# Hybrid layer with mixture-of-experts lookup: a second half of one token block leaves the dense up products, and 120 of 128 up tiles run early

## The chip, the cores and the metric

The kernel runs on one core of one Trainium2 chip. The metric is the device time of one execution in microseconds (us), median of several.

## The reference

One layer on 512 tokens of width 1024 in float32. A mixer (sliding-window attention, gated delta rule) and its output projection come first and are not touched here. Then comes the expert lookup, `peer`:

```python
q = (xt @ w_q).reshape(T, PEER_HEADS, 2, PEER_HALF)
s = jnp.einsum('thpc,hpnc->thpn', q, sub_keys)
s_top, i_top = lax.top_k(s, PEER_TOPK)
cand_s = s_top[:, :, 0, :, None] + s_top[:, :, 1, None, :]      # 16 x 16 sums
cand_i = i_top[:, :, 0, :, None] * N_KEYS + i_top[:, :, 1, None, :]
best_s, pos = lax.top_k(cand_s, PEER_TOPK)
idx, gate = take(cand_i, pos), softmax(best_s)
act = gelu(einsum('tkd,td->tk', u_tab[idx], x))
out = einsum('tk,tkd->td', act * gate, v_tab[idx])
```

Each token picks 8 x 16 = 128 of 16384 experts (128 x 128 pairs of keys i, j). Each expert is a row u and a row v of 1024 numbers.

## The kernel before, in words

The 512 tokens are four blocks of 128. Block 0 takes the way of single rows: for each of its 128 picks a gather brings [128 tokens, u and v] (1 MB, `Gathered.fetch`, line 1804), VectorE makes the dot with the token (`dot`, 1811) and, with gelu and gate, adds the scaled v row (`add`, 1828). Dots and adds are steps that `pair_steps` deals out, by a list of rates, to the batches of the routing stage and to the tiles of the last stage.

Blocks 1 to 3 take the dense way: all 128 x 128 experts' dots, with a gate of zero where an expert isn't picked. An **up tile** is the product of 128 u rows (one key j, all i) with the tokens; each operand is split in a high and a low part, so it is 8 x 3 matmuls. ScalarE makes the high part of u (`split_u`), GpSimd or VectorE the low part by subtraction (`u_low`, 2008), TensorE multiplies by the token columns (2097, 2098, then 2102 once the low part is there). A **down tile** is the product of gated activations with 128 v rows, 18 matmuls of 512 columns (2426 to 2428) over 384 tokens.

For half of block 1 (its first 64 tokens, NS = 64) the up dots don't come from the dense way but from gathered u rows (class `UpRows`): the 64 tokens' 128 picks are folded into 64 gathers of [128, 1024] (512 KB, 1878) and 64 VectorE dots (1885). The folding needs the second half of the indices and gates moved between partitions by two transfers (1868, 1869) and the tokens' rows repeated by a matmul (2125). Their activations times gates go in as the values of the gate matrix. So up tiles have 320 columns (TU = 384 - 64).

The work is three stages. The **routing stage** (about 408 to 905 us) runs the first FIRST = 27 up tiles (DRAM gets their gelus, 160 KB each) while VectorE selects the picks of blocks 1 and 2 (`Selection.part`, 13 parts a block; the order of blocks is 1, 2, 3, 0). Then 48 batches of 8 tokens build the gate matrix: VectorE writes two one-hots (2238), ScalarE scales one (2177), TensorE multiplies them (2119), ScalarE evicts and every second batch SP stores 1 MB. Between the two halves of a batch run more up tiles, `ups_in[n]`; in a batch VectorE also does a part of a selection (`beside`), the dots on gathered rows (DOTS = 2 a batch from batch 0), and from batch LATE = 32 steps of block 0. GpSimd goes in program order through `pool_low` (the subtractions) and the gathers; a gather into one of four row places waits until the dot that used the place is done. EARLY = 104 up tiles are made in this stage.

The **last stage** first runs its 24 up tiles beside down tiles (two tiles behind, a loop of three bodies of 8), then 104 down tiles alone, with gelus loaded back (L2370), v tiles in four places (2352) and gate tiles of 768 KB. Steps of block 0 run at 3.1 and then 1.5 a tile. At the end h is added and stored; h itself is loaded again in one transfer of 2 MB. SP issues all these loads in one order, each after the wait for its place.

The lines that set the order of a batch on TensorE and on GpSimd:

```python
for n in range(NB_):
    for i in range(BT // 4):
        for t in ups_of[n][i:i + 1]:
            up(t)
        gate_products(n, i)
```
```python
for n in range(LATE):
    for k in range(fetched, min(NS, fetched + (DOTS if n else 2 * DOTS))):
        up_rows.fetch(pool, k)
        fetched += 1
    for t in ups_of[n]:
        pool_low(t)
```

Of the kernel before, what the change touches and what calls it, by code (L numbers as in the profile page):

```python
# [51 lines left out]
EARLY = 104  # L52
NU = 4
TD = T - P
NS = 64
NR = P // NS
# [1242 lines left out]
class Selection:  # L1299
# [4 lines left out]
    def __init__(self, nc, sem, own, mem, scores, sgate, sidx):  # L1304
# [17 lines left out]
        self.idxf = part_of("top_index_f", [P, 2, PH, TOPK])  # L1322
# [9 lines left out]
        self.zsum = part_of("rt_z", [P, PH])  # L1332
        self.row0_made = part_of("row_starts", [P, TOPK])
        self.rowd = part_of("row_lengths", [P, TOPK])
        self.moved = part_of("shared_index_moved", [P, P], U32)
# [6 lines left out]
    def place_constants(self, dve, bank):  # L1342

        link = self.link(dve)
        self.iota, self.row0 = bank[:, 0:NK], bank[:, NK:NK + TOPK]
        self.step = bank[:, 256:512].rearrange("p (q h a) -> p q h a", q=2, h=PH)
        link(self.nc.vector.tensor_copy(self.iota, self.iota_made[:]))
        link(self.nc.vector.tensor_copy(self.row0, self.row0_made[:]))
# [7 lines left out]
    def second(self, r, w):  # L1356
        return self.top[:, 1, :, 0:w].unsqueeze(2).broadcast_to([P, PH, r, w])
# [7 lines left out]
    def constants(self, pool):  # L1365
# [14 lines left out]
    def part(self, dve, b, part):  # L1380
# [27 lines left out]
        elif part == 5:  # L1408
            off = 0
# [14 lines left out]
        elif part == 6:  # L1424
# [5 lines left out]
            link(nc.vector.tensor_copy(self.zsum[:].unsqueeze(2), self.best[:, :, 0:1]))  # L1430
            nc.vector.tensor_tensor(self.best[:], self.best[:], self.bc(self.zsum[:].unsqueeze(2), TOPK),
                                    ALU.subtract).then_inc(self.subbed, 1)
        elif part == 7:

            nc.vector.tensor_copy(self.posf[:], self.pos[:])
            link(nc.vector.tensor_copy(self.idxf[:], self.idx[:]))
            nc.vector.tensor_copy(self.step[:, :, :, 0:1], self.idxf[:, :, :, 0:1])
            link(nc.vector.tensor_tensor(self.step[:, :, :, 1:], self.idxf[:, :, :, 1:], self.idxf[:, :, :, :TOPK - 1],
# [5 lines left out]
            link(nc.vector.tensor_tensor(self.wide[:], self.flat(self.posf).unsqueeze(2).broadcast_to([P, HA, TOPK]),  # L1444
                                         self.row0.unsqueeze(1).broadcast_to([P, HA, TOPK]), ALU.is_ge))
        elif part in (8, 11):
            for h in range(PH):
                v = self.wide[:, h * TOPK:(h + 1) * TOPK, :]
                t = nc.vector.tensor_tensor(v, v, self.step[:, 0 if part == 8 else 1, h].unsqueeze(1)
                                            .broadcast_to([P, TOPK, TOPK]), ALU.mult)  # L1450
            link(t)
        elif part == 9:

            link(nc.vector.tensor_reduce(self.packed[:], self.wide[:], AX, ALU.add))
            link(nc.vector.tensor_copy(self.words[:], self.packed[:]))
            nc.vector.tensor_scalar(self.words2[:], self.words[:], 63, None, ALU.bitwise_and)
            link(nc.vector.tensor_scalar(self.words[:], self.words[:], 6, None, ALU.logical_shift_right))
            nc.vector.tensor_copy(self.small[:, 0, :], self.words[:])
            link(nc.vector.tensor_copy(self.column[:], self.words2[:]))
# [1198 lines left out]
```

## Time and profile before

| | |
|---|---|
| median of 3 runs | 1532.24 us (1531.07 to 1534.07) |
| the profiled execution | 1532.0 us, its span 1530.3 us |
| TensorE busy | 1451.6 us, 95% of the span |
| VectorE busy | 1275.8 us, 83% |
| ScalarE busy | 829.3 us, 54% |
| GpSimd busy | 504.4 us, 33% |
| DMA | 420.49 MB, mean 275 GB/s over the span |
| granted TensorE clock | 0.985 of full in the mean |

PE is TensorE, PEld its weight loads, DVE VectorE, ACT ScalarE, POOL GpSimd, SP the queue that issues most transfers. Busy times of PE count overlapping matmuls once. The DMA share is the time that packets took on the core's 16 DMA engines; it goes a little over 1 when packets of two queues overlap on an engine.

### The profile page before, as it was taken

The numbers are of one execution on the slowest core, as the hardware profiler recorded it, in microseconds if no ns is written. First come the engines' busy times: TensorE is split into PE (matmuls) and PEld (weight loads), VectorE is DVE, ScalarE is ACT, GpSimd is POOL, SyncE is SP. The second block draws the span as 40 slices with busy tenths as digits, with TensorE's granted clock in tenths as the row PEclk, the third lists the DMA queues.
The fourth block names the chain that finished last, engine by engine and source line by source line (L and its number), as shares of the span: only waits on it lengthen the run. The fifth ranks groups of instructions, "written<-read, shape, count | busy, mean of one in ns | idle before, by whom it ended". The sixth has DMA issues, their size and how long they took to land.

```text
span 1530.3 us, 25321 instructions
## 1 busy us (share of the span) xinstructions
PE 1451.6 (95%) x9438; PEld 1311.3 (86%) x9438; DVE 1275.8 (83%) x2444; ACT 829.3 (54%) x1571; POOL 504.4 (33%) x425
## 2 busy tenths in 40 slices
PE   7999699999999999999998989999989999999999
PEld 6898578779999999998998979999868888888887
DVE  4538778675799899999868949999979999998996
ACT  4453454133244667777767754444546565655653
POOL 4111620010177867776731103222212222221210
PEclk9999999999999999999999999999999999999999
DMA  5230001321266898999999999999999999999993
GB/s 185 93 98 1 8 30 61 135 97 70 75 192 231 283 321 301 346 340 311 334 353 386 384 350 352 380 380 324 386 408 410 410 409 411 409 411 409 410 390 105
DMA packets 168440, 420.49 MB, mean 275 GB/s; under 512 B 12897, under 2 KB 100097, under 8 KB 151681
## 3 DMA queue, kind: packets, MB, share of 16 engines
q1 hardware_dynamic: 125632, 234.06, 42.3%
q0 software_dynamic: 27712, 167.82, 28.3%
q10 hardware_dynamic: 14976, 17.05, 3.1%
q8 instruction: 73, 1.20, 0.3%
q14 instruction: 47, 0.38, 0.1%
HBM read 372.44 MB, written 46.40 MB: 274 GB/s over the span
## 4 chain that ended last, share of the span: by engine, by line
PE 47%; DVE 15%; DMA 6%; POOL 2%; issue 1%; ACT 1%; SPq 0%; ACTq 0%; DVEq 0%; POOLq 0%
PE bank L2426 7%; PE bank L2428 7%; PE bank L2427 7%; PE banks L2426 3%; PE banks L2428 3%; PE banks L2427 3%; PE bank L2102 3%; PE bank L2097 3%; PE bank L2098 3%; DVE pair_rows L1885 2%; DMA u_raw<-in_peer_u 2%; DVE onehot_i L2238 2%; DVE onehot_j L2238 2%; PE bank L2414 2%; PE bank L2415 2%; PE bank L2416 2%
## 5 line engine op out<-in xcount | busy, mean ns | idle before, releaser
L2097 PE MATMUL bank<-x_hi,u_split 128*128 128x320 f32 x832 | 253.4, 316 | 1.6 <-ACT u_split L2157 1.6
L2098 PE MATMUL bank<-x_lo,u_split 128*128 128x320 f32 x832 | 246.8, 309 | 0.0
L1804 POOL DMA_INDIRECT scores<-in_peer_uv,pair_index x86 | 106.3, 1236 | 389.0 <-DVE pair_sum L1828 387.9
L2473 ACT ACTIVATE act_tile<-onehots 128x384 f32<-128x384 f32 x128 | 124.3, 971 | 82.1 <-DVE act_lo L2515 78.4
L2097 PEld LDWEIGHTS bank<-x_hi,u_split 128*128 128x128 f32 x832 | 157.9, 190 | 2.6 <-issue 2.6
L2098 PEld LDWEIGHTS bank<-x_lo,u_split 128*128 128x128 f32 x832 | 157.2, 189 | 0.0
L2102 PE MATMUL bank<-x_hi,u_split 128*128 128x320 f32 x832 | 142.1, 312 | 13.2 <-POOL u_split L2008 13.2
L2102 PEld LDWEIGHTS bank<-x_hi,u_split 128*128 128x128 f32 x832 | 128.1, 190 | 15.3 <-POOL u_split L2008 15.3
L2008 POOL TENSOR_TENSOR u_split<-u_raw,u_split 128x1024 fp32r<-128x1024 f32 x41 | 98.8, 2412 | 79.9 <-DVE u_split L2008 58.2
L2426 PE MATMUL bank<-v_hi,act_hi 128*128 128x512 f32 x304 | 119.5, 393 | 1.5 <-DVE v_lo L2502 1.4
L2428 PE MATMUL bank<-v_hi,act_lo 128*128 128x512 f32 x304 | 119.1, 392 | 0.0
L2427 PE MATMUL bank<-v_lo,act_hi 128*128 128x512 f32 x304 | 118.3, 389 | 0.0
L2119 PE MATMUL bank<-onehot_j,onehot_gated 128*128 128x128 f32 x768 | 100.7, 279 | 13.4 <-ACT onehot_gated L2177 11.8
L1828 DVE SCALAR_TENSOR_TENSOR pair_sum<-scores,pair_c,pair_sum 128x1024 f32<-128x1024 f32 x86 | 110.1, 1282 | 1.5
L2502 DVE TENSOR_TENSOR v_lo<-v_raw,v_hi 128x1024 fp32r<-128x1024 f32 x76 | 92.7, 1220 | 21.4 <-ACT v_hi L2457 21.4
L2119 PEld LDWEIGHTS bank<-onehot_j,onehot_gated 128*128 128x128 f32 x768 | 96.1, 195 | 15.3 <-issue 14.2
L1804 POOL DMA_INDIRECT pair_rows<-in_peer_uv,pair_index x42 | 55.4, 1318 | 158.6 <-DVE pair_sum L1828 157.9
L2008 POOL TENSOR_TENSOR u_split<-u_raw_more,u_split 128x1024 fp32r<-128x1024 f32 x41 | 98.8, 2414 | 25.2 <-ACT u_split L2157 24.9
L1811 DVE SCALAR_TENSOR_TENSOR scores<-scores,mix 128x1024 f32<-128x1024 f32 x86 | 104.7, 1217 | 1.1 <-DMA scores<-in_peer_uv,pair_index 1.1
L2177 ACT ACTIVATE onehot_gated<-onehot_i,rt_smallT 128x128 f32<-128x128 f32 x320 | 101.3, 391 | 1.7 <-DVE onehot_i L2238 1.3
L2157 ACT ACTIVATE u_split<-u_raw_more 128x1024 fp32r<-128x1024 f32 x52 | 55.0, 1058 | 74.0 <-PE bank L2102 41.8
L2457 ACT ACTIVATE v_hi<-v_raw 128x1024 fp32r<-128x1024 f32 x76 | 80.0, 1053 | 23.1 <-DMA v_raw<-in_peer_v 22.8
(433 smaller groups left out, 4055.7 us busy)
## 6 DMA issues: line engine op xcount, KB each, us to landing
v_raw<-in_peer_v SPq DMA_DIRECT2D x128, 512.0 KB, 10.8
u_raw<-in_peer_u SPq DMA_DIRECT2D x64, 512.0 KB, 7.1
u_raw_more<-in_peer_u SPq DMA_DIRECT2D x64, 512.0 KB, 7.1
gates<-gate_stage SPq DMA_DIRECT2D x24, 1024.0 KB, 7.4
onehots<-gates SPq DMA_DIRECT2D x32, 768.0 KB, 11.4
early_gelus<-early_gelu ACTq DMA_DIRECT2D x104, 160.0 KB, 5.4
gelu_tile<-early_gelus SPq DMA_DIRECT2D x104, 160.0 KB, 11.2
w_raw<-in_w_in SPq DMA_DIRECT2D x9, 1024.0 KB, 5.2
```

The lines of the kernel that those rows point to most:

```text
L1804: pool.indirect_dma_start(self.slot(k), None, self.table, bass.IndirectOffsetOnAxis(ap=self.sidx[:, k:k + 1], axis=0)).then_inc(self.lande ...
L1811: self.nc.vector.scalar_tensor_tensor(row, row, 1.0, self.xn0, ALU.mult, ALU.mult, accum_out=self.s[:, at:at + 1]).then_inc(self.dots, 1)
L1828: self.nc.vector.scalar_tensor_tensor(total, self.slot(k)[:, D:], self.c[:, at:at + 1], total, ALU.mult, ALU.add).then_inc(self.summed, 1)
L2008: return on.tensor_tensor(ul[:, n % 2, :], u_raw[n % NU], uh[:, n % 2, :].bitcast(F32), ALU.subtract)
L2097: nc.tensor.matmul(out, uh[:, q, w], m.xh[:, k, P + NS:], start=(k == 0), stop=False)
L2098: nc.tensor.matmul(out, uh[:, q, w], m.xl[:, k, P + NS:], start=False, stop=False)
L2102: t = nc.tensor.matmul(out, ul[:, q, w], m.xh[:, k, P + NS:], start=False, stop=(k == KD - 1))
L2119: t = nc.tensor.matmul(banks.bank(g)[:, q * NK:(q + 1) * NK], og[:, n % RING, 4 * i + q, :], oj[:, n % RING, 4 * i + q, :], start=True, st ...
L2426: nc.tensor.matmul(bank[:], ah[:, s, w], v_hi[:, c], start=first, stop=False)
L2427: nc.tensor.matmul(bank[:], ah[:, s, w], v_lo[:, c], start=False, stop=False)
L2428: t = nc.tensor.matmul(bank[:], al[:, s, w], v_hi[:, c], start=False, stop=last)
L2473: nc.scalar.activation(af[n % 2][:], gt[:, it % 2, :, jj], ACT.Copy).then_inc(gate_cols, 1)
```

## The change

All 128 tokens of block 1 now take their up dots from gathered rows (NS = 128), so up tiles have 256 columns. Every token has a partition of its own, so the moving transfers, the repeated rows and the folding are gone; 128 gathers and 128 dots are made, five a batch in batches 0 to 24, through eight row places instead of four. 120 up tiles are early; 26 come before batch 0, batches 0 to 24 have three or two (67 in all), later ones one, four come last. In the selection several operands (places, packed words, the second keys' sums, the maximum) move from SBUF to PSUM, eight multiplications become one, some copies go. Block 2's picks are turned before batch 0, all 16 batches of block 1 come at the end. The four first v tiles are loaded in batches 40, 42, 44 and 46 instead of together at 32, and h in four parts.

The last stage keeps eight up tiles and has 120 down tiles alone; the steps of block 0 run at 1.7 a tile there. By the rates, 15 adds and 21 gathers of block 0 are placed in the routing stage both before and now; in the last stage 35 adds fell on the 24 up tiles and 78 on the 104 others, now 10 and 103.

```diff
-EARLY = 104
+EARLY = 120
-NS = 64
-NR = P // NS
+NS = P
...
-    LAST = 5
+    LAST = 4
     LATE = 2 * NBT
-    ups_in = [1 if n >= LATE or n % 4 == 3 else 2 for n in range(NB_)]
+    DOTS_FIRST, DOTS = 4, 5
+    LAST_DOT = (NS - 1 - DOTS_FIRST) // DOTS
+    ups_in = [1 if n > LAST_DOT else 2 if n % 3 == 2 else 3 for n in range(NB_)]
+    def ups_at(n, i):
+        return ups_of[n][0:1] if i == 0 else ups_of[n][1:]
...
-        beside[i * 29 // len(left)] = what
+        beside[i if i < sel.PARTS else sel.PARTS + (i - sel.PARTS) * 16 // sel.PARTS] = what
-    turned_at = {2: 1, 3: ready_at[3] + 1}
-    DOTS_FIRST, DOTS = 4, 2
+    turned_at = {2: -1, 3: ready_at[3] + 1}
-    COEFS = LAST_DOT + 2
+    COEFS = LAST_DOT + 4
+    V_AT = [NB_ - 8, NB_ - 6, NB_ - 4, NB_ - 2]
...
-                fetched = len(up_rows.slots)
+                SLOTS = len(up_rows.slots)
+                fetched = SLOTS - 2
                 for t in range(1, FIRST):
                     pool_low(t)
                     if t == TURN_1 + 2:
-                        up_rows.move(pool, sel)
-                    if t == TURN_1 + 3:
-                        up_rows.wait_moved(pool)
+                        pool.wait_ge(up_rows.chosen, 1)
                         for k in range(fetched):
                             up_rows.fetch(pool, k)
                 for n in range(LATE):
-                    for k in range(fetched, min(NS, fetched + (DOTS if n else 2 * DOTS))):
-                        up_rows.fetch(pool, k)
-                        fetched += 1
-                    for t in ups_of[n]:
+                    for i, t in enumerate(ups_of[n]):
                         pool_low(t)
+                        if i == 0:
+                            if n == 0:
+                                pool.wait_ge(sel.pairs_ready, 2)
+                            for k in range(fetched, min(NS, DOTS_FIRST + DOTS * n + SLOTS)):
+                                up_rows.fetch(pool, k)
+                                fetched += 1
...
-        self.iota, self.row0 = bank[:, 0:NK], bank[:, NK:NK + TOPK]
+        self.iota, self.posf, self.zsum = bank[:, 0:NK], bank[:, NK:2 * NK], bank[:, NK:NK + PH]
         self.step = bank[:, 256:512].rearrange("p (q h a) -> p q h a", q=2, h=PH)
+        self.packed, self.seconds = bank[:, 256:384], self.step[:, 1]
+        self.words = self.packed.bitcast(U32)
...
-            for h in range(PH):
-                v = self.wide[:, h * TOPK:(h + 1) * TOPK, :]
-                t = nc.vector.tensor_tensor(v, v, self.step[:, 0 if part == 8 else 1, h].unsqueeze(1)
-                                            .broadcast_to([P, TOPK, TOPK]), ALU.mult)
-            link(t)
+            v = self.wide[:].rearrange("p (h a) k -> p h a k", h=PH)
+            link(nc.vector.tensor_tensor(v, v, self.step[:, 0 if part == 8 else 1].unsqueeze(2)
+                                         .broadcast_to([P, PH, TOPK, TOPK]), ALU.mult))
...
         up_slots = [more[:, i, half * D:(half + 1) * D] for i in range(2) for half in range(2)]
+        up_slots += [rows[:, b, half * D:(half + 1) * D] for b in (1, 2) for half in range(2)]
-        rates = [2.0] * (P // 8) + [1.0, 2.0] + [3.1] * (NK - EARLY - 2) + [1.5] * EARLY
+        rates = [2.0] * (P // 8) + [1.0, 2.0] + [3.1] * (NK - EARLY - 2) + [1.7] * EARLY
...
+    H_AT = [NMT + 12 + 20 * b for b in range(TB)]
-                    if n == NMT + 4:
+                    if n in H_AT:
+                        b = H_AT.index(n)
                         sp.wait_ge(up_done, NMT)
-                        sp.dma_start(h[:], h_dram).then_inc(h_in, 16)
+                        sp.dma_start(h[:, b, :], h_dram[:, b, :]).then_inc(h_in, 16)
```

On GpSimd, in the batches: before, two gathers stood in a row, then the subtractions of one or two tiles (u_split is the tile of high and low parts, pair_rows and scores hold the row places; "x4" is four instructions in a row):

```order
L2008 TENSOR_TENSOR u_split<-u_raw,u_split 128x1024 [waits early_u_hi]
L1878 DMA pair_rows<-in_peer_uv,up_index 128x1024 [waits up_dots] x2
L2008 TENSOR_TENSOR u_split<-u_raw_more,u_split 128x1024 [waits early_u_hi] x2
L1878 DMA pair_rows<-in_peer_uv,up_index 128x1024 [waits up_dots] x2
L2008 TENSOR_TENSOR u_split<-u_raw,u_split 128x1024 [waits early_u_hi] x2
```

Now, from the last subtractions of batch 0 to the gathers of batch 2:

```order
L1989 TENSOR_TENSOR u_split<-u_raw_more,u_split 128x1024 [waits early_u_hi]
L1989 TENSOR_TENSOR u_split<-u_raw,u_split 128x1024 [waits early_u_hi] x2
L1856 DMA scores<-in_peer_uv,up_index 128x1024 [waits up_dots] x4
L1856 DMA pair_rows<-in_peer_uv,up_index 128x1024 [waits up_dots]
L1989 TENSOR_TENSOR u_split<-u_raw_more,u_split 128x1024 [waits early_u_hi] x2
L1989 TENSOR_TENSOR u_split<-u_raw,u_split 128x1024 [waits early_u_hi]
L1856 DMA pair_rows<-in_peer_uv,up_index 128x1024 [waits up_dots] x3
L1856 DMA scores<-in_peer_uv,up_index 128x1024 [waits up_dots] x2
```

Five gathers now stand together after the first subtraction of a batch, and up to three subtractions lie between two such groups.

On VectorE, batch 1 before (the one-hots, a selection part, two dots):

```order
L2238 TENSOR_TENSOR onehot_i<-bank,rt_smallT 128x1024
L2238 TENSOR_TENSOR onehot_j<-bank,rt_smallT 128x1024
L1393 MAX_INDEX top_index<-top,scores 128x8 x8
L1395 MATCH_REPLACE scores<-top,scores 128x128 x8
L1885 SCALAR_TENSOR_TENSOR pair_rows,up_s<-pair_rows,banks 128x1024 [waits rows_landed2,dve_in_order]
L1885 SCALAR_TENSOR_TENSOR pair_rows,up_s<-pair_rows,banks 128x1024 [waits rows_landed3]
```

and batch 1 now:

```order
L2222 TENSOR_TENSOR onehot_i<-bank,rt_smallT 128x1024
L2222 TENSOR_TENSOR onehot_j<-bank,rt_smallT 128x1024
L1387 MAX_INDEX top_index<-top,scores 128x8 x8
L1389 MATCH_REPLACE scores<-top,scores 128x128 x8
L1863 SCALAR_TENSOR_TENSOR pair_rows,up_s<-pair_rows,banks 128x1024 [waits rows_landed1,dve_in_order]
L1863 SCALAR_TENSOR_TENSOR pair_rows,up_s<-pair_rows,banks 128x1024 [waits rows_landed2]
L1863 SCALAR_TENSOR_TENSOR pair_rows,up_s<-pair_rows,banks 128x1024 [waits rows_landed3]
L1863 SCALAR_TENSOR_TENSOR scores,up_s<-scores,banks 128x1024 [waits rows_landed4]
L1863 SCALAR_TENSOR_TENSOR scores,up_s<-scores,banks 128x1024 [waits rows_landed5]
```

The batch has the same one-hots and the same selection part, and five dots where it had two.

## Rows read from the trace of the kernel before

**Rows 1.** The page: busy time of each engine, share of the span, instructions.

```profile
PE 1451.6 (95%) x9438; PEld 1311.3 (86%) x9438; DVE 1275.8 (83%) x2444; ACT 829.3 (54%) x1571; POOL 504.4 (33%) x425
```

**Rows 2.** Windows by stage: length, busy times, PEclk, DMA share, GB/s.

```profile
408.00:515.00 107.00, 103.03 (x681) 101.07 (x680) 97.87 (x383) 49.93 (x74) 75.46 (x38) 0.98 0.67 220
515.00:784.00 269.00, 259.52 (x1863) 257.94 (x1863) 249.84 (x648) 194.45 (x440) 190.47 (x117) 0.99 0.94 322
784.00:905.00 121.00, 104.69 (x746) 102.32 (x745) 94.20 (x104) 80.52 (x200) 14.79 (x15) 0.97 1.03 383
905.00:1090.00 185.00, 182.51 (x1001) 163.93 (x1000) 167.64 (x226) 92.08 (x143) 52.39 (x36) 1.00 0.95 358
1090.00:1140.00 50.00, 44.48 (x186) 36.01 (x185) 41.49 (x62) 24.72 (x36) 9.96 (x8) 0.93 1.02 412
1140.00:1490.00 350.00, 350.00 (x1532) 287.37 (x1531) 329.88 (x483) 208.86 (x291) 77.78 (x64) 1.00 1.02 408
1490.00:1530.00 40.00, 37.08 (x163) 30.14 (x161) 27.91 (x39) 13.35 (x19) 0.00 (x0) 1.00 0.32 114
```

**Rows 3.** DMA issues from 1140 to 1490 us: KB each, median us to landing.

```profile
v_raw<-in_peer_v SPq DMA_DIRECT2D x86, 512.0 KB, 12.1
```

**Rows 4.** Timeline of PE, 320 columns: start us, us, the instruction.

```profile
601.11 0.31 PE L2098 MATMUL bank<-x_lo,u_split 128*128 128x320 f32 x1
...
603.17 0.31 PE L2098 MATMUL bank<-x_lo,u_split 128*128 128x320 f32 x1
```

**Rows 5.** Timeline of PE, query projection at 256 columns.

```profile
362.08 0.28 PE L1558 MATMUL banks<-x_lo,w_oq_h 128*128 128x256 f32 x1
...
364.48 0.28 PE L1557 MATMUL banks<-x_hi,w_oq_h 128*128 128x256 f32 x1
```

**Rows 6.** Timeline of PE, down products at 512 columns.

```profile
1203.78 0.39 PE L2426 MATMUL banks<-v_hi_late,act_hi 128*128 128x512 f32 x1
...
1205.84 0.40 PE L2426 MATMUL bank<-v_hi,act_hi 128*128 128x512 f32 x1
```

**Rows 7.** Gate products: line 2119 (first and last start), then timeline, batch 32.

```profile
L2119 PE MATMUL bank<-onehot_j,onehot_gated x768: 271/275/550, 515.1 to 883.1; 128*128 128x128 f32 x192
...
784.34 1.95 PE L2119 MATMUL bank<-onehot_j,onehot_gated 128*128 128x128 f32 x16
```

**Rows 8.** Timeline of DVE and POOL: a copy at two places.

```profile
421.19 0.21 DVE L1430 COPY rt_z<-best 128x8 f32<-128x8 f32 x1
...
564.96 4.70 POOL L2008 TENSOR_TENSOR u_split<-u_raw_more,u_split 128x1024 fp32r<-128x1024 f32 x2
...
568.27 1.41 DVE L1430 COPY rt_z<-best 128x8 f32<-128x8 f32 x1
```

**Rows 9.** Timeline of DVE inside a batch: a dot and two one-hots.

```profile
562.39 1.22 DVE L1885 SCALAR_TENSOR_TENSOR pair_rows<-pair_rows,banks 128x1024 f32<-128x1024 f32 x1
...
563.53 1.22 DVE L2238 TENSOR_TENSOR onehot_i<-bank,rt_smallT 128x1024 f32<-128x1024 f32 x1
...
564.66 1.21 DVE L2238 TENSOR_TENSOR onehot_j<-bank,rt_smallT 128x1024 f32<-128x1024 f32 x1
```

**Rows 10.** Timeline of POOL: two gathers between u_low subtractions.

```profile
593.16 2.42 POOL L2008 TENSOR_TENSOR u_split<-u_raw,u_split 128x1024 fp32r<-128x1024 f32 x1 [0.30 <-ACT u_split L2157]
595.74 0.95 POOL L1878 DMA_INDIRECT pair_rows<-in_peer_uv,up_index  x1 [0.15 <-issue]
596.99 0.94 POOL L1878 DMA_INDIRECT pair_rows<-in_peer_uv,up_index  x1 [0.30 <-issue]
597.94 2.42 POOL L2008 TENSOR_TENSOR u_split<-u_raw,u_split 128x1024 fp32r<-128x1024 f32 x1
```

**Rows 11.** Windows of 10 us, same columns as rows 2.

```profile
590.00:600.00 10.00, 10.00 (x74) 10.00 (x73) 9.96 (x10) 7.99 (x19) 9.21 (x6) 1.00 1.01 372
1110.00:1120.00 10.00, 10.00 (x45) 8.19 (x45) 9.51 (x15) 4.97 (x7) 1.91 (x2) 1.00 1.02 421
```

More of the change, by code:

```diff
@@ L1408, in part @@
         elif part == 5:
+            link(nc.vector.tensor_copy(self.seconds, self.top[:, 1]))
             off = 0
@@ L1841, with __init__ @@
 class UpRows:
-    def __init__(self, nc, sem, slots, landed, xs, table, take):
+    def __init__(self, nc, sem, slots, landed, xs, table, strips):
         self.nc, self.slots, self.xs, self.table = nc, slots, xs, table
         self.landed = landed
-        self.chosen, self.moved, self.dots, self.gelus, self.coefs = (sem(n) for n in (
-            "up_chosen", "up_moved", "up_dots", "up_gelus", "up_coefs"))
-        self.idx, self.gate = take("up_index", [P, NS], U32), take("up_gate", [P, NS])
-        self.s, self.c = take("up_s", [P, NS]), take("up_c", [P, NR, NS])
+        self.chosen, self.dots, self.gelus, self.coefs = (sem(n) for n in (
+            "up_chosen", "up_dots", "up_gelus", "up_coefs"))
+        self.idx, self.gate = strips[0], strips[1]
+        self.s, self.c = strips[2], strips[3]
     def choose(self, dve, sel):
@@ L1981, in routing @@
             banks.add(("small", 1), "dve")
+    banks.add(("small", 2), "dve")
     for n, (b, k) in enumerate(BATCHES):
         for i in range(BT // 4):
-            for t in ups_of[n][i:i + 1]:
+            for t in ups_at(n, i):
                 banks.add(("up", t), "act")
@@ L2000, in routing @@
         smallT = sb("rt_smallT", [P, 2, 3, P])
-        ownT = sb("rt_ownT", [P, 3, NS])
+        ownT = [m.mem.over(f"own{i}", [P, NS], "x_hi", F32, 4 * T * i) for i in range(3)]
         small = sel.small
@@ L2434, in body @@
                         up(it, jj)
-                        if jj >= LAG or not isinstance(it, int):
-                            down(it * BODY + jj - LAG, jj - LAG + BODY, first=isinstance(it, int) and jj == LAG)
+                        if jj >= LAG:
+                            down(jj - LAG, jj - LAG, first=jj == LAG)
                 body(0)
-                with pe.Fori(1, NM) as it:
-                    body(it)
                 for n in range(NMT - LAG, NK):
@@ L2618, in hybrid_layer @@
         m.xs = two
-        up_rows = UpRows(nc, sem, up_slots, pairs_of_0.landed[:4], two[:].rearrange("p h d -> p (h d)"),
+        up_rows = UpRows(nc, sem, up_slots, pairs_of_0.landed + [sem(f"up_landed{i}") for i in range(2)], two[:].rearrange("p h d -> p (h d)"),
                          a["peer_uv"].rearrange("e (two d) -> (e two) d", two=2),
-                         lambda name, shape, dt=F32: mem.take(name, shape, dt))
+                         [mem.over(name, [P, NS], "x_hi", dt, 4 * T * (3 + i))[:] for i, (name, dt) in enumerate(
+                             [("up_index", U32), ("up_gate", F32), ("up_s", F32), ("up_c", F32)])])
         m.v_raw = [mem.over(f"v_raw{i}", [P, D], "selection", F32, 4 * D * i)[:] for i in range(3)]
```

120 lines of the change are left out of this document (48 added, 72 removed).

## The prediction, made before the changed kernel ran

> **What bounds the kernel now.** I read the page first. TensorE is busy 95% of the span and VectorE 83% [rows 1], so the question is which stage has room for work moved between engines. The windows by stage answer it [rows 2]. From 408 to 515 us (early up tiles and two selections) VectorE is busy 97.9 of 107 us and the DMA queues are at 0.67. From 515 to 784 us (batches 0 to 31) TensorE is busy 259.5 of 269 and DMA at 0.94. From 784 to 905 us DMA is at 1.03 and TensorE drops to 104.7 of 121: this stretch waits for loads. From 905 to 1090 us (24 up tiles beside down products) TensorE is nearly full. From 1140 to 1490 us (down products alone) TensorE is busy all 350 us, **and** DMA is at 1.02 with 408 GB/s. So the last stage has two bounds at once. Its v loads take 12.1 us in the middle from issue to landing [rows 3], with four places and a tile time near 4.1 us. A queue with room would not hold them so long.
>
> The start-to-start times of matmuls give TensorE's prices, since a row's own duration overlaps its neighbour. At 320 columns 14 matmuls take 603.17 - 601.11 = 2.06 us, 0.147 each [rows 4]; at 256 columns, in the query projection, 20 take 364.48 - 362.08 = 2.40 us, 0.120 each [rows 5]; at 512 columns nine take 2.06 us, 0.229 each [rows 6]. The first gate products of batch 0 start at 515.1 us and those of batch 32 at 784.3 [rows 7], 269.2 us or 8.4 a batch.
>
> **The change, part by part.**
>
> *Narrower up tiles.* 24 matmuls a tile: 24 x 0.147 = 3.52 us before, 24 x 0.120 = 2.88 after. For 128 tiles that takes 82 us off TensorE. It is worth time only where TensorE is what ends last.
>
> *The start.* TensorE now has 26 tiles ahead of batch 0 instead of 27, 26 x 2.88 = 75 us from about 411, plus some 5 us of waiting while GpSimd issues six gathers in a row (6 x 1.25 us, below), plus the first tile of batch 0: its first gate products could start at 494. VectorE must have finished block 2's selection by then. It ended at 515 with 9 us of idling in the window [rows 2], and now waits less, since six rows are fetched ahead. The copy of eight elements that takes 0.21 us alone took 1.41 us later, beside two GpSimd subtractions [rows 8]; the new PSUM operands take several such operations out of each selection, and the eight small multiplications become one. I put 12 us on both selections together, so about 494 as well. Taken: 495, a gain of **20** (between 10, if none of the long operations gets shorter, and 25).
>
> *Batches 0 to 24.* Here lies the price. The 64 further rows add 64 gathers of 512 KB (33.6 MB) and 64 VectorE dots. All 124 dots after the first four now come five to a batch, with 67 up tiles in 25 batches (2.68 each). Per batch:
> TensorE: 2.68 x 2.88 + 1.8 (16 gate-product records, [rows 7]) = 9.5 us.
> VectorE: two one-hots of 1.13 us, five dots of 1.14 [rows 9], and one part of a selection. Before, 32 batches held 249.8 us of VectorE work; less 64 one-hots (72.6) and 60 dots (68.4) that leaves 108.8 for 26 parts, 4.2 each with the long operations in it; I take 3.4. Sum 11.4, falling to about 10.8 from batch 13.
> GpSimd: u_low 2.41 us a tile, gathers 1.25 us from start to start and 0.95 for the last [rows 10]. With three tiles 3 x 2.41 + 0.15 + 4 x 1.25 + 0.95 = 13.3, with two 10.9; 17 and 8 batches give 12.5 in the mean, without one wait.
> DMA: 2.68 u loads (1.405 MB), five gathers (2.621), half a gate store (0.524), 2.68 gelu stores of 128 KB (0.351): 4.90 MB. At 372 GB/s, which ten saturated us of the same kind of traffic moved at a share of 1.01 [rows 11], it is 13.2 us; at the 421 GB/s of the best window shown, 11.6; at 322/0.94 = 343 GB/s, what rows 2 give per full share in batches 0 to 31, 14.3.
> So three resources lie between 11.4 and 13.2, and TensorE is no longer one of them. I take **13.0** a batch (ends: 12.5 from GpSimd, 14.3 from DMA): 325 us.
>
> *Batches 25 to 31* have one tile and no dot: 5.3 us each, as the one-tile batches after 784 had (3.52 + 1.78) before loads stopped them; 37 us. Batch 32 then starts at 495 + 325 + 37 = 857, against 784: **+73**, the 20 us of the start taken off.
>
> *Batches 32 to 47 and the last tiles.* DMA-bound [rows 2] and with almost the same bytes: 16 pair steps a side as before, one tile fewer at the end, narrower gelu stores (20 x 32 KB). The v tiles come at four places instead of one burst. 121 us become about 118: **-3** (0 to -8).
>
> *Up tiles in the last stage.* 24 x 3.52 = 84.5 us become 8 x 2.88 = 23.0: **-61.5**, all on TensorE's path, since rows 2 show it full from 905 to 1090. The spread reload of h ends the stop between 1090 and 1140 (44.5 busy of 50, clock 0.93), worth **-8** with its slow matmuls.
>
> *Down tiles.* 18 x 0.229 = 4.12 us of TensorE each, before and after. DMA per tile before: v 524 KB, gelu 164, an eighth of 1.57 MB of gates 197, and at 1.5 pair steps 0.75 gather of 1,049 KB, 786: 1.671 MB, 406 GB/s at that pace; the trace shows 408. After: gelu 131, and the steps 1.7 a tile, 0.85 gather, 891: 1.743 MB, which at 4.12 us would be **423 GB/s**. At the 408 GB/s of the long stretch a tile takes 4.27 us, 0.15 more, less the lead with which loads arrive early in the stage. About 115 tiles still load: **+17** (0 if 423 is carried; 50 at the 383 GB/s of 784 to 905, but there gate stores in pieces of 512 bytes ran too, which don't here, so I keep 25 as the end). VectorE was busy 329.9 of 350 us, 3.88 a tile; 0.2 step of 1.14 to 1.28 us more makes 4.1, less what the narrower gate product saves: it stays just under.
>
> The Trainium skill ("DMA: Bandwidth & Descriptors", Specifications) gives two ceilings: about 358 GB/s for HBM to one core, and 435 GB/s for the fabric. The first would make a down tile 4.87 us, and the trace disagrees: 408 GB/s for 350 us. The second would let 423 GB/s through, so the +17 would be nothing; no stretch here shows it, and what that would do is the first rival.
>
> Sum: 73 (which is -20 + 325 + 37 - 269) - 3 - 61.5 - 8 + 17 = +17 us on the span of 1530.3, and 1.7 around it: **1549 us**. The profiled execution took 1532.0, the median of the runs is 1532.2, so no correction.
>
> **The rivals.**
> *DMA has room (faster, 1519 us).* For it: TensorE never stopped from 1140 to 1490, and one window moved 421 GB/s. Against: a share of 1.02 and 12 us landings for 350 us. Place: down tiles stay at 4.12 (-17), and batches run at GpSimd's 12.5 (-13). It decides at about 423 GB/s of sustained rate. A small gain over before, since two thirds of the 61 us are spent on gathers.
> *GpSimd and TensorE take turns (slower, 1580).* Five gathers are 6 us in which no u_low is made; TensorE stands up to 4 us, and rows 2 show the clock below 1.00 wherever it stood. Slow matmuls delay the next high part, so GpSimd waits in turn: 14.2 us a batch, 25 x 1.2 = 30 more. Against: over 3 us of slack a batch on TensorE. It decides where the stop and the half-speed matmuls exceed that slack.
> *The narrow matmul isn't cheaper (1570).* A weight load is 0.19 us long and could set the pace. Rows 5 speak against it: 0.120 with a load before each. If it were so, 34 tiles on the path cost 0.64 us more each, 22 us.
>
> **How the numbers follow.** The forecast has 0.58, DMA with room 0.20, turns 0.19, no cheaper matmul 0.03. Within the forecast the ends of its terms (12.7 to 13.4 a batch, 10 to 22 in the last stage) give 1535 to 1562. 0.2%, about what a measurement of this kernel can tell from no change, is 3 us. Faster by more: 0.17 of the first rival and 0.07 of the forecast, 0.24; within: 0.08; slower: 0.68. The range takes in most of both rivals: 1520 to 1577.
>
> **What would show it.** First gate products at 495 and those of batch 32 near 857; DMA share about 1.0 and TensorE near 75% busy in batches 0 to 24; up matmuls 0.120 apart; the last stage some 53 us shorter, down tiles 4.25 us apart, v landing at 12 us or more. Wrong is the forecast if the batches come every 12 us or less, or down tiles every 4.12 us with over 415 GB/s.

## The result, and the profile after

The changed kernel takes **1563.1 us** (median of 4 runs, 1559.75 to 1565.75), the kernel before 1531.97 (4 runs, 1531.07 to 1534.07): a ratio of 1.02, 95% interval 1.0178 to 1.0222. It is slower, by 31 us; the forecast was 1549, within 1520 to 1577.

The page of the changed kernel (the line that answers to [rows 1]), and of its chain of waits the shares by engine and by line:

```profile
PE 1398.6 (90%) x9438; PEld 1242.1 (80%) x9438; DVE 1294.8 (83%) x2492; ACT 821.2 (53%) x1571; POOL 600.9 (39%) x502
...
DVE 23%; DMA 18%; issue 10%; ACT 8%; POOL 7%; PE 6%; SPq 1%; ACTq 1%; another core or an unknown queue 1%; DVEq 0%
DMA v_raw<-in_peer_v 9%; DMA u_raw<-in_peer_u 5%; DVE v_lo L2485 4%; POOL u_split L1989 4%; DVE scores L1801 3%; DVE v_lo_late L2485 3%; ACT u_split L2143 3%; DMA u_raw_more<-in_peer_u 2%; PE bank L2088 2%; DVE pair_sum L1818 2%; ACT onehot_gated L2163 2%; POOL pair_rows L1856 2%; DVE act_lo L2498 2%; DVE pair_rows L1801 2%; POOL scores L1856 2%
```

TensorE has 53 us less to do and the kernel takes longer. The chain, which ran through TensorE for 47% of the span before, now does so for 6% and runs through loads, subtractions and dots instead. The windows by stage, cut where the stages now lie (columns as in [rows 2]):

```profile
408.00:498.00 90.00, 80.47 (x658) 78.86 (x657) 85.06 (x334) 45.46 (x67) 71.01 (x35) 0.96 0.74 240
498.00:818.00 320.00, 259.80 (x2009) 253.74 (x2010) 283.01 (x735) 182.02 (x392) 272.81 (x188) 0.94 1.01 376
818.00:853.00 35.00, 33.91 (x287) 33.10 (x286) 26.71 (x26) 31.72 (x83) 17.88 (x10) 1.00 0.71 223
853.00:987.00 134.00, 103.72 (x786) 99.92 (x785) 101.70 (x115) 87.69 (x218) 15.92 (x17) 0.90 1.03 386
...
1240.00:1510.00 270.00, 262.65 (x1134) 210.98 (x1133) 252.45 (x374) 150.37 (x214) 68.53 (x54) 1.00 1.02 410
```

Batches 0 to 24 (498 to 818) hold TensorE busy 81% of the time, GpSimd 85%, VectorE 88%, DMA at 1.01. In the down products (last row) TensorE has gaps that it did not have before, at the same DMA rate, 410 against 408 GB/s. The ledger by stage, from the first starts of gate and down products in the two profiled executions (spans 1530.3 and 1558.0 us):

| | before | after | difference | forecast |
|---|---|---|---|---|
| first gate products, batch 0 | 515.1 | 498.6 | -16.5 | -20 |
| batches 0 to 24 | 214.4 | 319.7 | +105.3 | +110.6 (325) |
| batches 25 to 31 | 54.8 | 34.6 | -20.2 | -17.8 (37) |
| batch 32 to the first down product | 133.2 | 133.9 | +0.7 | -3 |
| the last stage, to the end | 612.8 | 571.2 | -41.6 | -52.5 |
| sum | | | **+27.7** | **+17** |

Batches 0 to 24 now take 319.7 / 25 = 12.8 us each, and batch 32 starts at 852.9 us instead of 784.3, 68.6 later.

### The profile page after: what moved, and what is told of

Same layout as the page of the kernel before. It is cut to its first block, busy times and chain, and to the rows that moved or that the text cites. A ratio compares the mean times of both kernels' runs of the same rounds, so it can differ in the third digit from the quotient of the medians.

```text
span 1558.0 us, 25442 instructions
## 1 busy us (share of the span) xinstructions
PE 1398.6 (90%) x9438; PEld 1242.1 (80%) x9438; DVE 1294.8 (83%) x2492; ACT 821.2 (53%) x1571; POOL 600.9 (39%) x502
## 4 chain that ended last, share of the span: by engine, by line
DVE 23%; DMA 18%; issue 10%; ACT 8%; POOL 7%; PE 6%; SPq 1%; ACTq 1%; another core or an unknown queue 1%; DVEq 0%
DMA v_raw<-in_peer_v 9%; DMA u_raw<-in_peer_u 5%; DVE v_lo L2485 4%; POOL u_split L1989 4%; DVE scores L1801 3%; DVE v_lo_late L2485 3%; ACT u_split L2143 3%; DMA u_raw_more<-in_peer_u 2%; PE bank L2088 2%; DVE pair_sum L1818 2%; ACT onehot_gated L2163 2%; POOL pair_rows L1856 2%; DVE act_lo L2498 2%; DVE pair_rows L1801 2%; POOL scores L1856 2%
## 5 line engine op out<-in xcount | busy, mean ns | idle before, releaser
L2083 PE MATMUL bank<-x_hi,u_split 128*128 128x256 f32 x960 | 250.6, 297 | 10.7 <-ACT u_split L2143 6.3
L2084 PE MATMUL bank<-x_lo,u_split 128*128 128x256 f32 x960 | 242.2, 288 | 1.5 <-issue 1.5
L2083 PEld LDWEIGHTS bank<-x_hi,u_split 128*128 128x128 f32 x960 | 191.1, 199 | 12.2 <-issue 9.1
L2088 PE MATMUL bank<-x_hi,u_split 128*128 128x256 f32 x960 | 142.6, 293 | 60.2 <-POOL u_split L1989 60.2
L2084 PEld LDWEIGHTS bank<-x_lo,u_split 128*128 128x128 f32 x960 | 190.3, 198 | 1.9 <-issue 1.9
L2088 PEld LDWEIGHTS bank<-x_hi,u_split 128*128 128x128 f32 x960 | 127.8, 198 | 65.4 <-POOL u_split L1989 65.3
L1989 POOL TENSOR_TENSOR u_split<-u_raw,u_split 128x1024 fp32r<-128x1024 f32 x49 | 118.0, 2409 | 82.0 <-DVE u_split L1989 58.2
L1989 POOL TENSOR_TENSOR u_split<-u_raw_more,u_split 128x1024 fp32r<-128x1024 f32 x50 | 119.8, 2401 | 16.9 <-ACT u_split L2143 16.4
L2143 ACT ACTIVATE u_split<-u_raw 128x1024 fp32r<-128x1024 f32 x61 | 64.3, 1056 | 84.6 <-PE bank L2088 34.1
L2413 PE MATMUL bank<-v_hi,act_lo 128*128 128x512 f32 x272 | 106.8, 393 | 0.0
L2412 PE MATMUL bank<-v_lo,act_hi 128*128 128x512 f32 x272 | 106.6, 392 | 0.0
L2411 PE MATMUL bank<-v_hi_late,act_hi 128*128 128x512 f32 x240 | 95.7, 399 | 6.2 <-DVE v_lo_late L2485 5.9
```

The lines of the kernel that those rows point to most:

```text
L1989: return on.tensor_tensor(ul[:, n % 2, :], u_raw[n % NU], uh[:, n % 2, :].bitcast(F32), ALU.subtract)
L2083: nc.tensor.matmul(out, uh[:, q, w], m.xh[:, k, P + NS:], start=(k == 0), stop=False)
L2084: nc.tensor.matmul(out, uh[:, q, w], m.xl[:, k, P + NS:], start=False, stop=False)
L2088: t = nc.tensor.matmul(out, ul[:, q, w], m.xh[:, k, P + NS:], start=False, stop=(k == KD - 1))
L2143: nc.scalar.activation(uh[:, n % 2, :], u_raw[n % NU], ACT.Copy).then_inc(u_hi if n < EARLY else nxt.u_hi_ready, 1)
L2411: nc.tensor.matmul(bank[:], ah[:, s, w], v_hi[:, c], start=first, stop=False)
```

## The experiments

**The parts of the change one by one.** Three kernels lie between before and after. The first is the kernel before with the PSUM operands alone; its edit is this and what belongs to it (the eight multiplications made into one and the dropped copies too):

```diff
+        self.iota, self.posf, self.zsum = bank[:, 0:NK], bank[:, NK:2 * NK], bank[:, NK:NK + PH]
...
+        self.packed, self.seconds = bank[:, 256:384], self.step[:, 1]
...
+            link(nc.vector.tensor_copy(self.seconds, self.top[:, 1]))
```

> The kernel before with the selection operands in PSUM alone; v tiles in one burst and h in one transfer as before. The variant with all small parts had batches 0 to 31 in 256.5 us instead of 269.2, and a last stage 4 us shorter. If the first comes from the selection and the second from the spread loads: batch 32 near 771 to 773 us and a last stage of 612 to 613, 1519 to 1522 us. If the spread v tiles gave the first part, batch 32 stays near 784 and the time near 1528 to 1531.

The second adds the four v tiles at batches 40 to 46 and h in four parts:

```diff
-                        for i in range(len(m.v_raw)):
...
+                    if n in V_AT:
+                        i = V_AT.index(n)
...
+                    if n in H_AT:
+                        b = H_AT.index(n)
...
+                        sp.dma_start(h[:, b, :], h_dram[:, b, :]).then_inc(h_in, 16)
```

> The kernel before, with only the small parts of the change: selection operands in PSUM (eight multiplications as one), the four v tiles spread over batches 40 to 46, h loaded in four parts. Still 64 rows by gathers, 320 columns, 104 early tiles. My theory (the cost of the change sits in the further gathers; these parts only help): first gate products at 504 to 508 us instead of 515, the stop between 1090 and 1140 us gone (about 6 us), so 1514 to 1522 us, 10 to 18 below before. Rival A (the small parts hurt too: PSUM reads collide with TensorE's writes, or the spread loads only move the wait): no gain, 1530 or more. If this gains and the changed kernel loses, the wider routing by gathers costs even more than its net +31.

The third has all of the change except the 16 further early tiles; its last stage has 24 up tiles in three bodies of eight again:

```diff
-EARLY = 120
+EARLY = 104
...
-    ups_in = [1 if n > LAST_DOT else 2 if n % 3 == 2 else 3 for n in range(NB_)]
+    ups_in = [1 if n > LAST_DOT else 2 for n in range(NB_)]
...
-        rates = [2.0] * (P // 8) + [1.0, 2.0] + [3.1] * (NK - EARLY - 2) + [1.7] * EARLY
+        rates = [2.0] * (P // 8) + [1.0, 2.0] + [3.1] * (NK - EARLY - 2) + [1.5] * EARLY
```

> The changed kernel with 104 early tiles instead of 120: two up tiles in each of batches 0 to 24, 24 up tiles of 256 columns in the last stage, rates 3.1 and 1.5 there. My theory (DMA near 1.0 sets batches 0 to 24, and DMA at some 410 GB/s sets the down tiles at 1.7 steps): a batch moves 4.45 MB instead of 4.90, so 11.6 to 12.1 us instead of 12.8, batch 32 near 836; down tiles alone at 4.12 us again (1.64 MB a tile), last stage about 590 us from a first down product near 967: 1550 to 1558 us in all. Rival B (128 columns fewer are a gain by themselves and only the 16 further early tiles hurt): 1532 or less. Rival C (five gathers in a row on GpSimd set the batch, not DMA): GpSimd's own sum falls from 12.5 to 10.9, so VectorE's 11.4 decides and a batch takes 11.0 to 11.4.

Measured, with the ratio to before and its 95% interval:

| kernel | median, us | ratio | batch 32 at | last stage |
|---|---|---|---|---|
| PSUM operands alone | 1520.26 | 0.9906 (0.9886 to 0.9926) | 772.3 | 612.1 |
| all small parts | 1517.59 | 0.9917 (0.9894 to 0.9939) | 771.3 | 608.8 |
| 128 rows, 104 early tiles | 1545.2 | 1.0099 (1.0077 to 1.0121) | 815.6 | 594.1 |
| the change | 1563.1 | 1.02 (1.0178 to 1.0222) | 852.9 | 571.2 |

The small parts gain 13 us, nearly all of it by the PSUM operands, whose gain is shown to lie in batches 0 to 31; the two small kernels' intervals overlap, so the spread loads' own 4 us (last stage 612.1 to 608.8) show in the profiles only. The rows of the second half block, with the narrower tiles that they allow, take the ratio from 0.9917 to 1.0099, some 28 us, and the 16 further early tiles take it from 1.0099 to 1.02, some 15 us. The start is a miss: with the small parts I expected 504 to 508 us, and both small kernels stayed at 515 (514.8, 515.1). The window from 408 to 515 us of the variant with all small parts shows why:

```profile
408.00:515.00 107.00, 103.14 (x681) 101.40 (x682) 88.29 (x354) 50.24 (x75) 75.74 (x38) 0.98 0.66 222
```

VectorE has 88.3 us of work there where it had 97.9, and TensorE as much as before, 103.1: with 320 columns TensorE sets the start. The kernel with 104 early tiles, which has 27 tiles of 256 columns ahead of batch 0 as before, starts at 499.6. So nearly all of the changed kernel's 16.5 us needs the narrower tiles, and its one tile less gives at most 1. Narrower tiles with the old selections were not tried; the old 97.9 us of VectorE alone would end at 408 + 97.9 = 506, an estimate, so the last part of the gain seems to need both.

What the PSUM operands gave is seen in VectorE's groups over batches 0 to 31. Of the kernel before, from 516 to 784 us:

```profile
L1449 DVE TENSOR_TENSOR selectors<-selectors,bank 128x256 f32<-128x256 f32 x32 | 10.9, 410 | 0.0
...
L1411 DVE TENSOR_TENSOR sums<-top 128x128 f32<-128x128 f32 x2 | 6.2, 3094 | 0.0
L1435 DVE CAST best_place_f<-best_place 128x128 f32<-128x128 uint32 x2 | 5.7, 2848 | 0.0
...
L1455 DVE CAST packed_words<-packed 128x128 uint32<-128x128 f32 x2 | 4.0, 2004 | 0.1
```

and of the variant with PSUM operands alone:

```profile
L1445 DVE TENSOR_TENSOR selectors<-selectors,bank 128x2048 f32<-128x2048 f32 x4 | 9.1, 2278 | 0.0
...
L1450 DVE CAST bank<-bank 128x128 uint32<-128x128 f32 x2 | 0.6, 300 | 0.1
...
L1408 DVE TENSOR_TENSOR sums<-top,bank 128x128 f32<-128x128 f32 x2 | 0.6, 289 | 0.1
```

Operations of the same size fall from 2 to 3 us to 0.3: the addition and the two casts shown took 15.9 us together and take about 1.8. The multiplications (first line of each), 32 made into 4, save 1.8 us of VectorE's time (10.9 to 9.1). The run has both at once, but most of what VectorE is spared comes from the operands. TensorE's waits for GpSimd's subtractions in these batches went from 9.5 us to 1.6, and its clock from 0.99 to 1.00.

The kernel with 104 early tiles came out below my band. Its batches 0 to 24 take 282.0 us, 11.3 each, what rival C gave and not the DMA theory's 11.6 to 12.1. Its window over them:

```profile
500.00:781.00 281.00, 215.37 (x1602) 209.69 (x1600) 278.84 (x731) 161.13 (x360) 233.97 (x170) 0.90 1.03 390
```

VectorE is busy 278.8 of 281 us: with two tiles a batch its sum decides. And the queues carry 390 GB/s, more than the 376 of the changed kernel. So the changed kernel's 376 GB/s was not the most that the queues can carry in such batches, and a second question followed: what holds the changed kernel's batches at 12.8?

**Batches 0 to 24: GpSimd, DMA, or their order.** Four variants of the changed kernel. The first halves the bytes of the gathers from the ninth on, with all instructions kept; it leaves out half of each row:

```diff
-        pool.indirect_dma_start(self.slots[k % n], None, self.table, ...
+        half = self.slots[0].shape[1] // (2 if k >= n else 1)
+        pool.indirect_dma_start(self.slots[k % n][:, 0:half], None, self.table if k < n else self.table4, ...
```

> The changed kernel with gathers 8 to 127 of block 1 fetching 512 numbers a partition instead of 1024 (and of other experts; the rest of each row place keeps old numbers): same instructions on every engine, 31 MB less to move. A batch of 0 to 24 then moves 3.6 MB instead of 4.9. GpSimd theory (its 12.5 us a batch decide, DMA adds only 0.3): batches at 12.4 to 12.6 us instead of 12.8. DMA theory with GpSimd's sum overestimated: 12.2 or less. Both give a gain in the span of 5 to 15 us, if nothing else takes it.

The second halves GpSimd's subtractions in these batches and leaves out half of the low part:

```diff
-                    u_low(nc.gpsimd, t).then_inc(low_by_pool, 1)
+                        c = slice(0, D // 2)
+                        nc.gpsimd.tensor_tensor(ul[:, t % 2, c], u_raw[t % NU][:, c], ...
```

> The changed kernel with GpSimd subtracting only 512 of 1024 columns for the up tiles of batches 0 to 24 (the other half of the low part is left out, its place holds an older tile's): GpSimd's sum falls from 12.5 to about 9.3 us a batch, transfers, VectorE and TensorE as before. DMA theory (4.9 MB at 376 to 383 GB/s): batches stay at 12.6 to 12.8 us, span within 5 us of 1558. GpSimd theory: VectorE's 11.4 or DMA at the 390 GB/s that the variant with 104 early tiles carried (12.5) comes next, so 11.4 to 12.5 us a batch, span 10 to 30 us lower.

The third has both edits:

> Both of the last two edits together: half the subtraction and half the bytes of the gathers in batches 0 to 24. GpSimd's sum is 9.3 us, DMA's 3.6 MB at 376 GB/s 9.5 us, TensorE's 9.5 us, VectorE's 11.4 falling to 10.8. Expected: VectorE decides, 11.0 to 11.5 us a batch, span 30 to 40 us below 1558. If batches stay at 12.5 or more, it is neither GpSimd nor DMA but the chain from one engine to the next.

The fourth takes nothing away and changes the order of gathers and subtractions alone:

```diff
...
-                            for k in range(fetched, min(NS, DOTS_FIRST + DOTS * n + SLOTS)):
...
+                        due = min(NS, DOTS_FIRST + DOTS * n + SLOTS)
+                        for k in range(fetched, due - (due - fetched) * (len(ups_of[n]) - 1 - i) // (len(ups_of[n]) - i)):
```

> The changed kernel with the five gathers of a batch dealt out behind its two or three subtractions (1, 2, 2 or 2, 3) instead of all behind the first. Nothing is taken away. Theory (GpSimd's sum and DMA set the batch, the order does not): 12.5 to 12.8 us a batch, 1555 to 1563 us in all, with TensorE waiting less than the present 54 us for low parts. Rival (the 6 us in which no low part is made, and the slow clock behind them, cost time): 12.0 to 12.3 us a batch, 1545 to 1553 us.

Windows over batches 0 to 24 (columns as in [rows 2]). With half the bytes:

```profile
499.00:818.00 319.00, 261.44 (x2003) 256.37 (x2003) 285.02 (x732) 182.27 (x392) 274.17 (x187) 0.92 0.85 278
```

With half the subtraction:

```profile
498.00:818.00 320.00, 258.47 (x2005) 252.12 (x2004) 280.13 (x729) 180.18 (x390) 201.76 (x187) 0.92 1.00 375
```

With both halves:

```profile
497.00:784.00 287.00, 251.20 (x2005) 246.35 (x2004) 279.84 (x732) 179.91 (x389) 201.49 (x187) 0.95 0.92 308
```

With the gathers spread:

```profile
497.00:808.00 311.00, 257.20 (x2008) 247.53 (x2008) 283.92 (x733) 182.03 (x394) 275.05 (x188) 0.96 1.03 387
```

| variant | batches 0 to 24, us | one | time |
|---|---|---|---|
| the change | 319.7 | 12.8 | 1563.1 |
| half the bytes | 320.2 | 12.8 | 1557.1 (one run) |
| half the subtraction | 321.0 | 12.8 | 1557.7 (one run) |
| both | 288.0 | 11.5 | 1523.1 (one run) |
| gathers spread | 311.6 | 12.5 | 1547.96, ratio 1.0107 (1.0074 to 1.014) |

This is what two limits at nearly the same height look like. Without a quarter of GpSimd's work (272.8 to 201.8 us busy) the batches stay at 12.8, with the queues at a share of 1.00; with a quarter of the bytes gone (a share of 0.85 in place of 1.01) they stay at 12.8 as well, with GpSimd as busy as before (274.2). The waits from 500 to 800 us (total, times, longest) say who waits in each case. GpSimd waits for a high part in the changed kernel

```profile
POOL u_split L1989 <- ACT u_split L2143: 9.7, 16, 1.0
```

and with half the subtraction, where ScalarE in turn waits for up loads:

```profile
POOL u_split L2050 <- ACT u_split L2148: 78.0, 35, 8.4
...
ACT u_split L2148 <- DMA u_raw<-in_peer_u: 33.4, 6, 7.5
...
ACT u_split L2148 <- DMA u_raw_more<-in_peer_u: 21.9, 2, 14.4
```

With half the bytes GpSimd's wait is 8.1 us and ScalarE's for up loads 6.6, where it is 55.3 with half the subtraction and 35.2 in the changed kernel. So in the changed kernel GpSimd hardly ever waits: its own sum is what ends last, and once it is shortened the up loads come too late. Only both edits together release the batches, and then VectorE (279.8 of 287) stands at 11.5, near the 11.3 of the kernel with 104 early tiles. Three of these are single runs, but the stage differs little between kernels that are alike in it (319.7 us in the changed kernel, 316.4 and 318.8 in the two variants of the last stage below), so 288 us is far outside and 320 to 321 within it or near. Half the bytes was a miss: both theories had 12.6 us or less. With half the subtraction the DMA theory's 12.6 to 12.8 came, and with both the expected 11.0 to 11.5.

The order is worth 0.3 us a batch, and my theory that it wouldn't matter is refuted by the time: it had 1555 us or more. TensorE's main wait from 500 to 800 us (total, times, longest), of the changed kernel:

```profile
PE bank L2088 <- POOL u_split L1989: 52.0, 22, 3.9
```

and with the gathers spread:

```profile
PE bank L2088 <- POOL u_split L1989: 38.2, 32, 1.9
```

The stops are shorter, the granted clock is 0.96 instead of 0.94, and the queues carry 387 GB/s instead of 376. GpSimd waits 2.9 us for high parts from 500 to 800 us instead of 9.7. The batches come every 12.46 us, which is GpSimd's own sum (12.5 in the prediction), so they weren't as fast as the rival's 12.0 to 12.3, though the whole came to the rival's 1545 to 1553. Of the 11.7 us between the spans (1558.0 and 1546.3), 8.1 fall on batches 0 to 24, the rest lies before and behind them (1.8 us at the start, 2.9 between batch 25 and the first down product, 1.1 given back in the last stage).

**The down products: DMA or VectorE.** The first variant leaves out the loads of gelus behind the fourth, the second leaves out half of each dot of block 0:

```diff
-                    if NMT <= n + NG2 < NK:
+                    if NMT <= n + NG2 < NMT + NG2:
```

> The changed kernel, whose last stage reads the gelus of the first four early tiles only and uses them for all others: 116 loads of 128 KB left out, no other instruction on any engine changed. A down tile then moves 1.61 MB instead of 1.74. DMA theory: tiles back at 4.12 to 4.16 us instead of 4.35, at 388 to 392 GB/s, span 18 to 26 us below 1558. VectorE theory (its 1.7 steps a tile, 4.1 us busy in theory, set the pace): tiles stay at 4.30 to 4.35 us, span within 5 us of 1558.

```diff
-        row, at = self.slot(k)[:, 0:D], k % (2 * GRP4)
+        row, at = self.slot(k)[:, 0:D // 2], k % (2 * GRP4)
```

> The changed kernel with the dots of block 0 made over 512 of the 1024 columns (the other half of these sums is left out); all transfers as before. VectorE loses about 0.85 x 0.55 = 0.47 us a down tile. DMA theory: tiles stay at 4.30 to 4.35 us and 410 GB/s, span within 5 us of 1558. VectorE theory: tiles at 4.12 to 4.2 us, span 15 to 26 us lower.

From 1240 to 1510 us, without the gelu loads:

```profile
1240.00:1510.00 270.00, 269.06 (x1171) 218.94 (x1170) 261.76 (x390) 155.72 (x223) 68.86 (x53) 1.00 0.98 384
```

and with half dots:

```profile
1240.00:1510.00 270.00, 261.00 (x1131) 210.84 (x1130) 225.91 (x376) 150.36 (x214) 57.34 (x54) 1.00 1.02 409
```

Without 7.5% of the bytes TensorE is full again. The last stage takes 552.3 us instead of 571.2, or, less eight up tiles of 2.88 us, 4.135 a down tile instead of 4.283; before it was (612.8 - 84.5) / 128 = 4.127. The other 7.6 us between the spans (1531.5 and 1558.0) arose ahead of the first down product, where the edit changes nothing; that start lies at 979.2 us here, 986.8 in the changed kernel and 990.7 with half dots, three kernels that are alike up to batch 32, so it moves by several us from run to run. These 7.6 us are therefore not put down to the gelus. With half dots VectorE has 26.5 us less to do in these 270 us (225.9 for 252.4) and all transfers stay: the last stage takes 570.9 us, the same as the changed kernel's. The DMA theory holds: fewer bytes bring the pace back and less VectorE work doesn't. The pace, 4.283 us for 1.743 MB, is 407 GB/s.

**A way past both kernels.** The waits that deal the first six gathers of block 0 to batches 32 to 34, from the changed kernel, put into the variant with all small parts:

```diff
                 for k in range(nxt.fetched):
+                    if 2 <= k < len(pairs_of_0.slots):
+                        pool.wait_ge(oj_ready, LATE + k // 2)
```

> The kernel before with the small parts, and of the changed kernel also the waits that let the first six gathers of block 0 (1 MB each) go two at a time, beside batches 32 to 34, instead of in a row. In the variant without it TensorE stopped for 8.3 us near 795 us behind an up load that landed 10.8 us late. Theory (the burst of 6 MB delays that load): the stop shrinks to under 3 us, 1510 to 1515 us. Rival (the stretch from 771 to 870 is bound by DMA in the mean, so a stop removed in one place comes back in the next): 1516 to 1519 us.

It took 1517.79 us, ratio 0.99 (0.9878 to 0.9922): the rival's time, no further gain over the small parts. The waits from 780 to 806 us show why:

```profile
ACT u_split L2155 <- DMA u_raw_more<-in_peer_u: 11.1, 1, 11.1
PEld bank L2117 <- issue: 8.8, 1, 8.8
PE bank L2117 <- ACT onehot_gated L2175: 8.7, 1, 8.7
```

and SP's queue there:

```profile
779.89 0.38 SPq L2033 DMA_DIRECT2D gates<-gate_stage  x1
780.31 12.95 SPq L2024 DMA_DIRECT2D u_raw<-in_peer_u  x1
793.31 0.50 SPq L2024 DMA_DIRECT2D u_raw_more<-in_peer_u  x1
```

The stop is still there (8.7 us). SP sat 12.95 us at one issue of an up load, a few batches after the subtractions go over from GpSimd to VectorE. The queues had no room in the time of the stop:

```profile
784.00:794.00 10.00, 3.22 (x24) 3.03 (x23) 2.22 (x3) 1.39 (x3) 0.40 (x1) 0.80 1.03 404
```

The burst of gathers wasn't its cause. That the stretch is bound by DMA, as the rival has it, fits the share of 1.03, but no run shows which transfer the late load stood behind. Both this and the variant with all small parts are faster than either kernel of the study; no difference between them can be measured.

## Why the prediction was right, and where its sizes were off

*The sign.* Right for its reason: TensorE's saving was paid for in batches 0 to 24 by gathers, and part of the last stage's gain was lost to DMA.

*The start, -20:* it was -16.5. The prediction had both engines reach 494. The small kernels show that shorter selections alone move nothing there; the narrower tiles carry the gain, and whether they would have given all of it without the selections is open.

*Batches 0 to 24, 13.0 each:* 12.8. That three resources lie close together was right, and the chosen value was near, but it was chosen between two ends: the measured 12.8 is GpSimd's 12.5, the lower end, and 0.3 of waits. What the working missed is that GpSimd and DMA meet at 12.5 to 12.8, so that relief of one alone is worth nothing. VectorE's term, 11.4 falling to 10.8, measured 11.3 and 11.5 where it decided. TensorE's 9.5 was 10.4 (259.8 / 25), at a granted clock of 0.94 in the mean: it was busy 81% of the time and not 75%. Batches 25 to 31 took 34.6 us for 37. Together +68.6 for +73.

*Batch 32 to the first down product, -3:* +0.7. The stretch is DMA-bound before and after, as said, and one batch of 12.2 us (860.5 to 872.7) stands in it among others of 5 to 8, as one of 15.5 did before.

*Up tiles in the last stage, -61.5:* borne out. In the kernel with 104 early tiles, 24 tiles at 2.88 instead of 3.52 (15.4 us) and the spread loads (about 4) give 19.4, and its last stage is 18.7 us shorter.

*The stop at 1090 to 1140, -8:* this term failed in size. The small parts show 3 to 4 us, 612.8 or 612.1 against 608.8.

*Down tiles, +17:* this is the term that was sized too small. With -61.5 and -4 the last stage should be 547.3 us; it is 571.2, so they cost **+24**, as my end of 25 had it. I took 4.27 us a tile and the loads' lead as a help; the low parts of v now come at most 1.5 us ahead of TensorE in most of the stage, where it was 3 to 7 before, so there was little lead to use up. Of the 24 us, 18.9 are undone by leaving out the gelus' bytes. Down products from the 24th to the 126th start 4.35 us apart on average, in stretches of 4.12 between others of 4.4 to 4.9. The window over the slowest stretch of the changed kernel shows TensorE with gaps and a clock under 1.00, and the queues at 386 GB/s with a share of 0.99; why they carry less than 407 there is open:

```profile
1188.00:1228.00 40.00, 36.98 (x156) 29.92 (x156) 35.00 (x52) 21.86 (x32) 9.40 (x8) 0.96 0.99 386
```

*The matmul's price* held. Two starts apart, 602.94 and 603.06, are 0.12 us as [rows 5] had it:

```profile
602.94 0.28 PE L2084 MATMUL bank<-x_lo,u_split 128*128 128x256 f32 x1
603.06 0.28 PE L2083 MATMUL bank<-x_hi,u_split 128*128 128x256 f32 x1
```

*The rivals.* DMA with room is refuted for down tiles: 410 GB/s is what they carried, where 423 were needed. The turns between GpSimd and TensorE were there, 52 us of TensorE's waits and a clock of 0.94, but cost 0.3 us a batch (the spread order gives them back), not 1.2. The cheaper matmul held (0.120), so the third rival falls. On the Trainium skill's two ceilings ("DMA: Bandwidth & Descriptors", Specifications), 358 and 435 GB/s: this trace again shows 408 to 410 for hundreds of us.

*The sum.* +17 in the forecast, +27.7 in the profiled spans, +31 in the medians, whose own spread is 6 us. The terms off are -4.4, +3.7 and +10.9, the last of them DMA in the down tiles and the overrated stop.

## What to carry to other kernels

Before work is moved off a bound engine, add up every engine and queue of the stage it goes to. Where two of them end within some per cent of the new sum, halve both together in an experiment: halved one at a time each looks innocent. A stage where TensorE and DMA are both full has no room for a saving on one of them, so take the bytes away first. And try the small parts of a large change alone: here they were the only gain.

## What the hardware showed beyond expectation

On VectorE two casts of 128x128 from SBUF to SBUF took 2.0 and 2.85 us in the mean in batches 0 to 31, and an addition of two SBUF operands 3.09; with PSUM on one side or both, 0.3 and 0.29. They wait for GpSimd and do not run slower. In the kernel before, the cast that starts at 598.15 us ends 0.09 us after the subtraction of GpSimd that was under way:

```profile
598.15 2.29 DVE L1455 CAST packed_words<-packed 128x128 uint32<-128x128 f32 x1
...
597.94 2.42 POOL L2008 TENSOR_TENSOR u_split<-u_raw,u_split 128x1024 fp32r<-128x1024 f32 x1
```

With its operands in PSUM it runs in the middle of such a subtraction:

```profile
706.50 0.30 DVE L1450 CAST bank<-bank 128x128 uint32<-128x128 f32 x1
...
705.71 2.42 POOL L2002 TENSOR_TENSOR u_split<-u_raw_more,u_split 128x1024 fp32r<-128x1024 f32 x1
```

In the kernel before, from 408 to 784 us, 14 casts, copies and products or sums of at most 128 numbers a partition in the selection took over 1 us, and all ended so, 0.03 to 0.15 us behind a subtraction of GpSimd. The longest (4.04 and 4.07 us) sat through two subtractions in a row. A cast inside SBUF that met none is short (line 1459, 0.22 us). And the PSUM variant still has one product with both operands in SBUF that meets a subtraction, 2.58 us for the 0.28 that it took before:

```profile
729.15 2.58 DVE L1469 SCALAR_TENSOR_TENSOR pair_column<-rt_small 128x128 f32<-128x128 f32 x1
...
729.17 2.41 POOL L2002 TENSOR_TENSOR u_split<-u_raw_more,u_split 128x1024 fp32r<-128x1024 f32 x1
```

The Trainium skill ("SBUF — State Buffer", Who interferes with whom) says that of VectorE and GpSimd the second to come waits for the whole instruction, if VectorE's runs in a two-port mode (which copies and casts inside SBUF can) or has two inputs in SBUF. The trace agrees: operations with one operand in PSUM did not wait. It adds that the wait can go on through the next GpSimd instruction. In the prediction I put the gain into the selections ahead of batch 0, when it was worth 12 us in the batches.

In batches 0 to 24 the DMA queues carried 376 GB/s at a share of 1.01, 387 at 1.03 when the same gathers were issued in another order, and 390 with 104 early tiles. So a share of 1.0 doesn't fix the rate: there it stood beside 376 to 390 GB/s, in the down products beside 410.
